# A hybrid attention decoder step: the sample's selective heads read their chosen keys alone

## The reference, cut to what matters

```python
def select_keys(scores, qpos, n_keys, topk):
    causal = kpos[None, None, :] <= qpos[None, :, None]
    _, idx = lax.top_k(jnp.where(causal, scores, -jnp.inf), topk)
    ...
def dsa_sample(qa, ka, va, qi, ki, wi, cache_k, cache_v, cache_ik, page_table, bias_a):
    past = page_table.shape[1] * cache_k.shape[1]                     # 32 pages of 128 keys: 4096
    ki_all = jnp.concatenate([gather_pages(cache_ik, page_table), ki], axis=1)
    idx, valid = select_keys(indexer_scores(qi, wi, ki_all), qpos, n_keys, min(TOPK_MAX, n_keys // 4))
    k_sel = gather_selected(cache_k, page_table, ka, idx, past)       # 256 keys for each query token
    v_sel = gather_selected(cache_v, page_table, va, idx, past)
    return dsa_core(qa, k_sel, v_sel, valid, qpos[None, :, None] - idx, bias_a)
```

## Time and profile before

| | |
|---|---|
| runs, median (lowest to highest) | 2460.18 us (2459.58 to 2466.08) |
| the profiled execution: its span, from first to last instruction | 2590.7 us |
| TensorE busy | 2312.3 us, 89% |
| VectorE, ScalarE, GpSimd busy | 43%, 30%, 25% |
| granted TensorE clock over the span | 0.951 |
| the stage of the change, on the span's scale | about 565 to 1339 us |
| its B chunks, its A chunks | about 647 to 1150, 1150 to 1336 |

### The profile page before, as it was taken

One profiled execution on the slowest core, in us unless ns is written; L12 is line 12 of the kernel. 1 busy time (PEld: TensorE's weight loads), 2 busy tenths in 40 slices (PEclk: granted clock), 3 DMA queues, 4 the chain that ended last, 5 costly groups with the idle time before them and its releaser, 6 DMA issues. The chain is left out here.

```text
span 2590.7 us, 32530 instructions
## 1 busy us (share of the span) xinstructions
PE 2312.3 (89%) x12169; PEld 1549.6 (60%) x12189; DVE 1103.6 (43%) x2687; ACT 766.2 (30%) x2065; POOL 660.5 (25%) x703
## 2 busy tenths in 40 slices
PE   7999997767777878788789898899999999999999
PEld 5644443443455455555444445548888888888887
DVE  5489998742445533333322212352443343371001
ACT  3551345653444444444421013311111111110000
POOL 1451223123544445433301010013222121201110
PEclk9999998988889889998889999999999999999999
DMA  4211101025888778765540014111111111122221
GB/s 140 73 60 70 38 9 65 1 82 188 275 277 269 234 266 281 257 213 193 173 162 28 33 49 163 34 67 34 50 34 50 34 50 40 44 65 74 74 63 39
DMA packets 147603, 281.75 MB, mean 109 GB/s; under 512 B 13479, under 2 KB 82775, under 8 KB 147447
## 3 DMA queue, kind: packets, MB, share of 16 engines
q0 software_dynamic: 48384, 176.18, 20.2%
q1 hardware_dynamic: 80774, 90.50, 10.6%
q10 hardware_dynamic: 18288, 12.98, 1.7%
HBM read 261.68 MB, written 17.94 MB: 108 GB/s over the span
## 5 line engine op out<-in xcount | busy, mean ns | idle before, releaser
L634 PE MATMUL PS<-region 128*128 128x512 f32 (+5 forms) x864 | 327.7, 534 | 1.8 <-DMA region<-w_in 1.8
L2784 PE MATMUL PS<-region,ffn_w 128*128 128x264 f32 x1408 | 323.1, 388 | 1.6 <-PEq L2234 1.6
L2784 PEld LDWEIGHTS PS<-region,ffn_w 128*128 128x128 f32 x1408 | 269.2, 191 | 48.4 <-issue 1.9
L2004 ACT COPY region<-PS 128x512 f32<-128x512 f32 x352 | 197.2, 591 | 212.6 <-PE PS L1868 72.2
L634 PEld LDWEIGHTS PS<-region 128*128 128x128 f32 (+1 forms) x864 | 152.7, 181 | 161.2 <-issue 140.9
L2784 PE MATMUL PS<-region,side 128*128 128x264 f32 x1056 | 245.0, 389 | 1.8 <-POOL side L2741 1.8
L1875 PE MATMUL PS<-ident_f,region 128*128 128x128 f32 x1024 | 170.7, 316 | 82.4 <-ACT region L2004 44.1
L2784 PEld LDWEIGHTS PS<-region,side 128*128 128x128 f32 x1056 | 200.0, 191 | 35.8 <-POOL side L2741 1.9
L1875 PEld LDWEIGHTS PS<-ident_f,region 128*128 128x128 f32 x1024 | 133.5, 162 | 117.0 <-issue 76.3
L931 DVE TENSOR_SCALAR_CACHE_REDUCE mask<-score,cand 128x384 bf16<-128x384 f32 (+2 forms) x198 | 180.9, 942 | 3.4
L1109 POOL DMA_INDIRECT region<-cache_b_k,gather_b x128 | 120.4, 941 | 212.0 <-PE PS L1875 177.8
(11 more groups left out here) (448 smaller groups left out, 4017.7 us busy)
## 6 DMA issues: line engine op xcount, KB each, us to landing
ffn_w<-w_gate SPq DMA_DIRECT2D x11, 1024.0 KB, 5.4
ffn_w<-w_up SPq DMA_DIRECT2D x11, 1024.0 KB, 5.5
region<-w_in SPq DMA_DIRECT2D x4, 2048.0 KB, 7.9
ffn_w<-w_down ACTq DMA_DIRECT2D x7, 704.0 KB, 5.6
region<-x_prompt ACTq DMA_DIRECT2D x8, 512.0 KB, 7.1
region<-x_prompt SPq DMA_DIRECT2D x8, 512.0 KB, 10.6
mem_keys<-cache_mem_k SPq DMA_DIRECT2D x8, 512.0 KB, 5.0
mem_values<-cache_mem_v SPq DMA_DIRECT2D x8, 512.0 KB, 8.0
```

Source lines behind the costliest of these rows:

```text
L634: last = nc.tensor.matmul(M.PS[0:n, s % 3, 0:chunks[j].width], XT[:, c, t * P:t * P + n], w[j % 2][:, c, 0:chunks[j].width], start=(c == 0 ...
L2004: nc.scalar.copy(dst, M.PS[0:dst.shape[0], T0 + x % 2, 0:dst.shape[1]]).then_inc(t_read, 1)
L2784: last = nc.tensor.matmul(M.PS[:, bank, 0:TW], left[:, c, :], right[:, c, :], start=begin and c == 0, stop=(c == KH - 1), skip_group_check ...
```

## The change

After the bisection the kernel now lists the chosen keys. 41 further steps, z, follow the 33 c. Step 0 multiplies the 0/1 picture of the chosen keys (`work`, 128x1024: four segments of 1024 keys on the partitions 32 seg + token) with each key's row number in the pool plus 1. In 32 rounds VectorE takes the eight highest of a partition (`max`) and strikes them out (`match_replace`), both over 128x1024. Then the four segments' lists are shifted by how many there are before them, bit by bit, and one matmul sums them into 256 row numbers for each token. There are three c or z steps in a chunk, and z weighs nothing in `beside`, c 0.5, a step of the A chunks 2.

The A part has two chunks for a group, of 4 x 512 keys: 256 chosen keys for each of 4 x 4 tokens (chunk 0: tokens 0 and 1 of each sequence, chunk 1: tokens 2 and 3; the mask keeps a row to its own token's keys), and one chunk for the last page (128 keys) and the new keys, with the old mask and the bias. The chosen keys of the last page are left out of the lists. Each chunk of chosen keys is a "set": 16 gathers of keys and 16 of values, each 128 rows of 512 bytes. The last page takes 16 more.

The diff, cut to its core:

```diff
         selective = [n for n, (kind, g, c) in enumerate(walk.chunks) if kind == "A"]
         order = beside(walk.steps, a_steps,
-                       lambda step: 0.5 if step[0] in "kspof" and step[1] in selective else 1.0, lambda step: 1.0)
+                       lambda step: {"c": 0.5, "z": 0.0}.get(step[0], 2.0 if step[0] in "kspof" and step[1] in selective
+                                                             else 1.0), lambda step: 1.0)
 
...
+
     def __init__(self):
         self.chunks = []
-        for kind, n_chunks in (("B", NCB), ("A", HALVES * NCA)):
+        for kind, n_chunks in (("B", NCB), ("A", 2)):
...
             keys = [("k", n + 1, j) for j in range(1 if self.new(n + 1) else 4)] if n < end else []
-            self.steps += keys[:3] + [("p", n)] + keys[3:] + [("o", n)] + [("c", r) for r in itertools.islice(cut, 1)]
+            self.steps += keys[:3] + [("p", n)] + list(itertools.islice(cut, 1)) + keys[3:] + [("o", n)]
+            self.steps += list(itertools.islice(cut, 1))
             if n < end:
-                self.steps += [("s", n + 1)] + [("c", r) for r in itertools.islice(cut, 1)]
+                self.steps += [("s", n + 1)] + list(itertools.islice(cut, 1))
             if self.new(n):
                 self.steps.append(("f", n))
         self.news = [n for n in range(end + 1) if self.new(n)]
...
-        x = walk.turn(u, j) % 6 if u >= walk.first_a else j
-        return (kv[:, 4 + x, :], loaded[4 + x]) if x < 4 else (apart[x - 2], M.gathered_apart[x - 2])
+        return (apart[j], M.gathered_apart[j]) if walk.aside(u) else (kv[:, 4 + j, :], loaded[4 + j])
+
+    def set_keys_at(x, j):
+
+        if x == 0:
+            return rel[:, 0, j * CH:(j + 1) * CH]
+        if x == 1:
+            return apart[j // 2][:, j % 2 * CH:(j % 2 + 1) * CH]
+        return kv[:, (0 if x == 2 else 4) + j, 0:CH]
+
+    def set_values_at(x, j):
+
+        if x == 0:
+            return (M.X[:, 8, 0:CH], M.kdi[:], spare[:, 0, :], spare[:, 1, :])[j]
+        if x == 1:
+            return apart[2 + j // 2][:, j % 2 * CH:(j % 2 + 1) * CH]
...
+        def near(b):
+            gather(near_k[:, b, :], near_loaded, kv_rows["A", 0], M.gather_n, b)
+            gather(near_v[:, b, :], near_loaded, kv_rows["A", 1], M.gather_n, b)
+
+        def chosen(x, v, j):
+
+            out, arrived = (set_values_at(x, j), set_values[x]) if v else (set_keys_at(x, j), set_keys[x])
+            for q in range(4):
+                t, half = 2 * (x % 2) + q // 2, q % 2
+                gather(out[:, q * P:(q + 1) * P], arrived, kv_rows["A", v], ids,
+                       half * NS + DEC_T * (4 * (x // 2) + j) + t)
+
+        last = walk.n_units - 1
+        nc.gpsimd.iota(iota[:], [[1, PAGE]], base=1, channel_multiplier=0).then_inc(iota_made, 1)
         for h, g in ((0, 1), (1, 0), (1, 1)):
                 for j in range(4):
                     if (h, g) == (1, 1):
...
+            keys(u)
             values(u)
-            if u == walk.first_a + 2:
-                eng.wait_ge(o_ss, 1)
-                nc.gpsimd.tensor_scalar(oms[:], oss[:], 1.0 / (2 * HD), EPS, ALU.mult, ALU.add).then_inc(o_ms, 1)
-                eng.wait_ge(o_ms, 1)
-                nc.gpsimd.tensor_tensor(ors[:], oms[:], M.neg_half[0:NS, 0:4], ALU.pow).then_inc(o_rs, 1)
+            if u == last - 5:
+                eng.wait_ge(listed, 2)
+            if last - 5 <= u < last - 3:
+                for b in range(4 * (u - last + 5), 4 * (u - last + 5) + 4):
+                    near(b)
+            if last - 3 <= u <= last:
+                for j in range(2 * ((u - last + 3) % 2), 2 * ((u - last + 3) % 2) + 2):
+                    chosen(0, (u - last + 3) // 2, j)
+        used(last - 2)
+        for v in range(2):
+            for j in range(4):
+                chosen(1, v, j)
+        for j in range(4):
+            turned(last, j)
+            chosen(2, 0, j)
+        for j in range(4):
+            chosen(2, 1, j)
+        used(last)
+        for v in range(2):
+            for j in range(4):
+                chosen(3, v, j)
+        eng.wait_ge(o_ss, 1)
+        nc.gpsimd.tensor_scalar(oms[:], oss[:], 1.0 / (2 * HD), EPS, ALU.mult, ALU.add).then_inc(o_ms, 1)
+        eng.wait_ge(o_ms, 1)
+        nc.gpsimd.tensor_tensor(ors[:], oms[:], M.neg_half[0:NS, 0:4], ALU.pow).then_inc(o_rs, 1)
 
     def sync(eng):
...
+                eng.wait_ge(t_full, fill["k", walk.sets[0], 3, 0] + 1)
             else:
-                eng.wait_ge(pv_done, walk.units[-1] + 1)
+                eng.wait_ge(pv_done, walk.sets[1] + 1)
...
+            if r == 0:
+                eng.wait_ge(iota_made, 1)
+                link(nc.vector.tensor_copy(iota_f[:], iota[:]))
+                link(nc.vector.tensor_tensor(score[:, 0:SEGW].rearrange("p (n c) -> p n c", c=PAGE),
+                                             M.page_rows[:].unsqueeze(2).to_broadcast([P, SEGW // PAGE, PAGE]),
+                                             iota_f[:].unsqueeze(1).to_broadcast([P, SEGW // PAGE, PAGE]), ALU.add))
...
+                link(nc.vector.tensor_tensor(work[:, 0:SEGW], work[:, 0:SEGW], score[:, 0:SEGW], ALU.mult))
+            elif r <= walk.ROUNDS:
+                eight = lists[0][:, 8 * (r - 1):8 * r]
+                link(nc.vector.max(eight, work[:, 0:SEGW]))
+                link(nc.vector.match_replace(work[:, 0:SEGW], eight, work[:, 0:SEGW], 0.0))
+            elif r == walk.ROUNDS + 1:
...
+                                                          b[:, far:TOPK], ALU.mult, ALU.add)
+                    if k == 7:
+                        last.then_inc(shifted, 1)
+                    else:
+                        link(last)
+            elif r == walk.LISTED:
+                eng.wait_ge(t_read, fill["z", walk.ROUNDS + 7] + 1)
+                link(nc.vector.tensor_scalar(slots_f, slots_f, -1.0, 0.0, ALU.add, ALU.max))
+                nc.vector.tensor_copy(ids[:], slots_f).then_inc(listed, 1)
+                link(nc.vector.tensor_scalar(list_f, list_f, 0.0, NEG, ALU.is_equal, ALU.mult))
+                nc.vector.tensor_tensor(mask[0:NS, 0:SEGW].rearrange("p (t x) -> p t x", t=DEC_T),
+                                        list_f.unsqueeze(1).to_broadcast([NS, DEC_T, TOPK]),
+                                        K("tok_mask").unsqueeze(2).to_broadcast([NS, DEC_T, TOPK]), ALU.add
+                                        ).then_inc(listed, 1)
...
```

More of the change, by code:

```diff
@@ L1589, in __init__ @@
         self.news = [n for n in range(end + 1) if self.new(n)]
[L1590 to L1592 removed]
+        self.n_units = sum(kind == "B" and c >= 0 for kind, g, c in self.chunks)
+        self.units = [n for n, (kind, g, c) in enumerate(self.chunks) if kind == "B" and c >= 0]
+        self.sets = [n for n, (kind, g, c) in enumerate(self.chunks) if kind == "A" and c >= 0]
         self.fill, x = {}, 0
@@ L1604, in new, with near @@
         return self.chunks[n][2] < 0
+    def near(self, n):
+        return self.new(n) and self.chunks[n][0] == "A"
     def first(self, n):
@@ L1653, in fills @@
             return [x + (j,) for x in self.index if self.turned_at(x) == step for j in range(4)]
-        if step[0] == "k" and not self.new(step[1]):
+        if step[0] == "k" and (not self.new(step[1]) or self.near(step[1])):
             return [step + (x,) for x in range(2 if self.chunks[step[1]][0] == "B" else 1)]
+        if step[0] == "z":
+            return [step] if step[1] in (self.ROUNDS + 2, self.ROUNDS + 7) else []
         return [step] if step[0] in "pc" else []
@@ L1882, in logits @@
             out = M.PS[:, L0, 0:w]
-            if not walk.new(n):
-                eng.wait_ge(t_read, fill["k", n, 3, 1 if kind == "B" else 0] + 1)
+            if not walk.new(n) or walk.near(n):
+                eng.wait_ge(t_read, walk.last_turned(n) + 1)
             if n:
@@ L1961, in outputs, with list_kept @@
             last.then_inc(pv_done, 1)
+        def list_kept(step):
+            if step not in fill:
+                return
+            if step[1] == walk.ROUNDS + 2:
+                eng.wait_ge(counted_kept, 1)
+                t = bank(step)
+                nc.tensor.matmul(t[:, 0:1], K("seg_before"), count[:, 0:1], start=True, stop=True).then_inc(t_full, 1)
+                return
+            eng.wait_ge(shifted, 1)
+            t = bank(step)
+            for half in range(2):
+                nc.tensor.matmul(t[:, half * NS:(half + 1) * NS], lists[0][:, half * P:(half + 1) * P],
+                                 K("seg_sum")[:, 0:NS], start=half == 0, stop=True, skip_group_check=half > 0)
+            nc.tensor.matmul(t[0:NS, 2 * NS:2 * NS + TOPK], K("seg_sum")[:, 0:NS], lists[0], start=False, stop=True,
+                             skip_group_check=True).then_inc(t_full, 1)
         for g in range(2):
```

266 lines of the change are left out of this document (160 added, 106 removed).

## The result

The changed kernel takes 2498.37 us (median of 4 runs, 2494.04 to 2503.48), the kernel before 2463.03 in the same job (median of 4, three of which are the runs listed ahead of the prediction): ratio 1.0148, 95% interval [1.0121, 1.0176]. It is slower by 35 us where 32 us less were forecast. The changed kernel's profiled span is 2495.5 us, close to its runs; that of before in the earlier trace rows was 5.3% over its own.

The account below looks back on a forecast made before the run. The prediction took transfers to bound the B chunks and GpSimd's queue the part from unit 27 on. -46.7 + 5 (TensorE) + 8 (rounds) = -33.7 us, scaled to -32, gave 2428 us from 2460.2; range 2403 to 2478.

Parts of the forecast that it names:

- So the B chunks go at the pace of the transfers: B chunks: eight gathers of 524 KB at 266 GB/s take 15.8 us, a chunk 15.9, so transfers set the pace.
- I scale: Whole kernel: the runs' median is 0.950 of the profiled span, so -33.7 us of the profile becomes -32.
- the sum along GpSimd: From unit 26's last gather to the stage's end: GpSimd's issues and waits added up, ending at 1292 instead of 1338.8, -46.7 us.
- the rounds: VectorE, chunks 11 to 21: 2.5 us a round, three a chunk fit in 10.5 free us; 8 us lost, bounds 0 and 40.
- Issues at 1.24: GpSimd's queue: each small gather starts 1.24 us after the one before, as large ones do; bounded below by 0.94.
- The wait for unit 31's values: GpSimd, before unit 31's values: a wait of 9 us for the chunk just before, bounds 3 and 17.
- the tail: End of the stage: landing 1.9 us, 14 us behind the last values, then the barrier's 3.6 us.
- VectorE's rounds bind: Rival, chunks 11 to 21: rounds of 4.6 us make chunks 19.2 us against 15.9; +18 us scaled, 2478 us; chance 0.14.
- Gathers by the piece: Rival, GpSimd's queue: each small gather holds it for its landing, 1.9 us instead of 1.24; +58 scaled, 2518 us; chance 0.08.
- TensorE's 5 us: Between the last sets: about 17.5 us of TensorE's fixed-order work in 20 us; 5 us for what doesn't fit, bounds 0 and 12.
- TensorE decides: Rival, A part: if issues cost 0.94 us without the gap of 0.30, the stage ends 102 us sooner; 2363 us; chance 0.07.
- The third count step: Chunks 0 to 10: costs nothing, as transfers cover it; without that cover 1.3 us in 11 chunks, 14 us.

Follow-up runs that it names:

- before_again: The kernel before, unchanged, run for a second profile: median 2463.91 us, 0.9996 of the kernel before.
- no_rounds: The changed kernel without the 32 rounds of max and match_replace, so its lists hold other row numbers: 2466.93 us, 1.0016 of the kernel before.
- even: The changed kernel with four count steps in a chunk, then rounds and shifts three and two in turn: 2502.37 us, 1.0182 of the kernel before.
- half_sets: The changed kernel with 8 instead of 16 gathers of keys and of values for sets 1 to 3: 2464.99 us, 1.0006 of the kernel before.
- before_rounds: The kernel before plus 32 rounds of max and match_replace on an unread buffer, three a chunk from chunk 17: 2484.68 us, 1.0095 of the kernel before.
- few_no_rounds: The changed kernel without max and match_replace and without 112 of the sets' 128 gathers: 2416.77 us, 0.9837 of the kernel before.

## Why the prediction was wrong

**The step that failed is the base: "So the B chunks go at the pace of the transfers", and "I scale".** The profile of before is 130.5 us over the runs, and the prediction spread this over the whole (0.950). The stages behind this one take 1251.9 us in it and 1253.3 in `before_again`; this stage took 774 us there and 654 in `before_again`. So 120 us lay in it alone: 79 in stretch I, 37 in II, 4 ahead of them. The reading "at 266 GB/s that is 1.97 us each, 15.8 us for the eight" could not find this out, since 266 is those bytes over those 15.9 us: it would fit whatever set the pace. The `remote` waits stood in the same view as the earlier trace rows. Against a stretch of 304.6 us the sum along GpSimd gives -46.7; against the 267.6 of `before_again` it gives -9.7. With this base alone put right, the prediction's own terms are -9.7 + 5 + 8, about +3 us: no gain, but not the +35 measured either. The second failed term is the rounds.

**GpSimd's sum in stretch II** held in its terms. Forecast 257.9 us, with the 5 for TensorE 262.9, measured 270.7. Issues at 1.24: measured 1.25. Units 27 to 30 at 19.8: their first gathers are 19.9 to 20.2 us apart (985.0, 1005.2, 1025.1, 1045.2, 1065.4). The wait for unit 31's values, 9: 11.7. From unit 26's last gather to the start of the stage's last it was 243.7 us, forecast 237.2 (1272.6 less one issue). The rest is the tail, 27.0 us for some 20.6. Of these 6.4 us 3.3 lie between the last gather's start and the matmul that uses it (6.4 us for 3.1), where TensorE is at work on the prompt's V and L; 1.6 up to VectorE's last addition (15.6 for 14), where T went at half speed; and 1.5 in the barrier (5.1 for 3.6). So II lost 3 us against the kernel before, where -46.7 had been counted: 37.0 by the base, 12.8 by the sum.

**The rounds** cost 2.52 us each as taken, but 31 to 35 us of the whole and not 8. "10.5 of 15.9 us are free" rested on the same profile. At the 12.8 us a chunk of `before_again` 7.4 are free, and three rounds take 7.6. In `no_rounds` a chunk takes 11.9 us and VectorE's work in it is 6.0 (83.8 in 14), so less still is free. The rival "VectorE's rounds bind" had the place and the mechanism right, with its condition (3.8 us a round at 15.9 us a chunk) wrong for the same reason. Its 2478 is 20 us off, as is the 2518 of *Gathers by the piece*, whose nearness is luck. That density matters is shown by `even`: a round costs half as much at 2 and 3 a chunk. Why 13.6 us are left (179.6 against 166.0) stays open; that a round delays the maximum or T behind it even where VectorE has room was not tried by itself.

**TensorE's 5 us** between the last sets was right in kind: GpSimd decides there in the changed kernel, and half_sets shows TensorE just behind it. *Gathers by the piece* has the wrong mechanism, since issues stayed 1.25 us apart; *TensorE decides* needed the gaps gone, and they stayed. The third count step, put at nothing, goes with 7 us more (chunks 0 to 10: 126.5 us against 119.7, with 136 and 140 matmuls of the prompt in them); four, together with 4 rounds, with 20 more. No run varied the count step alone.

**The balance**, on profiles: I +23.8 (rounds +34.9, all else in it -11.1), II +3.1, together 26.9 us, and 5.3 less outside, so the spans differ by 21.7. The medians differ by 35.3. The profiled execution of `before_again` (2475.61) is 11.7 us over the median of its own runs, which is most of the gap; its A chunks are 7.6 us longer than the same ones in `before_rounds`. By the fifth column of the table: without rounds and set gathers the change is worth -41 us (few_no_rounds), the rounds cost 30.5, the 112 set gathers 48.7, together 38 where 35.3 were measured.

## What to carry to other kernels

A profile that is 5% over its runs must first be asked where its excess lies; a second profile of the same kernel tells it at once, and every free share read in that stage is too large until then. A rate is no proof of what sets the pace, since it is worked out from the time that it is to explain: look instead at how long the transfers' engines are busy, and at waits that nothing recorded explains. Bytes saved are worth nothing where they are paid for by the instruction: 24 MB less came with 80 more issues of 1.25 us on a queue that then set the end. A step spread over an in-order engine is free only while its own work and the added fit the pace of the chunk. Look at each stretch of an experiment and count what lies in it, since `even` gained 18 us and lost 20 in neighbouring ones, and had moved 4 rounds from one to the other.

## What the runs showed of the hardware

- An indirect gather of 128 rows occupies GpSimd for 0.94 us and starts 1.25 us behind the one before, with rows of 512 bytes as with 4 KB; at the median those of 512-byte rows land 2.5 us after issue, those of 4 KB rows 5.4 to 6.3. In the last part 64 gaps between small gathers sum to 19.5 us, 0.30 each.
- `max` over 128x1024 float32 takes 1220 ns, `match_replace` 1209 ns and 92 ns for loading its eight values.
- Two profiled executions of the same program took 254 and 206 us for the same 16 chunks (266 and 326 GB/s), with the stages behind them within 2 us and the median 4 KB packet at 159 ns in both. The longer one has waits for TensorE that end up to 4.9 us behind its last recorded work.
- TensorE was granted 0.99 in chunks 11 to 24 without the rounds (busy for 0.89), 0.91 with them (0.80), and 0.80 in the last part (0.59); in `before_again` it was granted 0.95 at 0.90 busy, so the busy share alone does not tell it. At the lower of its two clocks 16 transposes took 3.62 us and 32 matmuls 3.68, where at the higher they took 1.91 and 1.97.
